# Two-stage transformer kernel: the late half of each attention unit moves to the end of its step

## The chip, the cores and the metric

The kernel runs on one core of a Trainium2 chip. The metric is the device time of one execution in microseconds (us), taken as the median of several runs.

## What is computed

The input is a sequence of 512 vectors of 1024 features. Two layers of a first block are applied (with 16 extra tokens in front, so 528), then two layers of a second block. Cut to what the change touches:

```python
# block 1, per layer: 4 heads of differential attention, causal, beside a recurrent branch
s = einsum('bqhcd,bkhcd->bhcqk', q, k) * scale          # two score maps c = 0, 1 per head
p = softmax(where(qpos >= kpos, s, -inf))
a = p[:, :, 0] - lam * p[:, :, 1]
o = einsum('bhqk,bkhe->bqhe', a, v)
h = h + concat([norm(o), norm(recurrent)]) @ w_out;  h = h + (silu(g) * u) @ w_down
# block 2, per layer: convolution, 6 heads of top-k attention (d), 6 heads of banded attention (c)
p = softmax(s + mask_or_bias);  y = einsum('bhqk,bkhd->bqhd', p, v)
x = layer_norm(ALPHA * x + concat([conv, y_d, y_c]) @ w_out)
# then attention over a memory of 256 tokens, and an MLP, each with a layer norm
```

## The kernel before, in words

**Products.** Activations are held with the features on the partitions. Every dense product is done as three float32r matmuls: high part of the weights by high part of the input (L511), low weights by high input (L514), high weights by low input (L517), in `dense` (L504). The weights arrive by DMA on the SP queue in pieces, ScalarE rounds the high part (`split_hi`, L985), VectorE subtracts the low part (`split_lo`, L1474), three buffers deep.

**Five programs and a table of steps.** Each engine has its own program, written out by hand; they meet through semaphores alone, and every engine works its list strictly in the order written. In the attention stage all five programs walk the same numbered steps, `STEPS1` = 80 steps in block 1 and steps 16 to 112 in block 2. In steps 0 to 63 of block 1 TensorE does in each step two chunks of an input projection (12 matmuls of 264 columns), in steps 64 to 66 and 75 to 79 chunks of the output projection, and in steps 67 to 74 no product at all. In block 2 a step holds 6 matmuls of 512 columns (steps 16 to 91), and from step 92 on the products for the memory's values, which call the units through `units` (L826).

**Units.** A unit is one block of 128 queries of one head (block 1: `UNITS1`, 20 per layer) or of one pair of heads (block 2: `UNITS2`, 24 per layer). They begin every 2 or 3 steps. A unit that begins at step s goes through the engines like this:

- step s: TensorE scores (L634, L636; L777, L779, L783 in block 2), VectorE maximum and its negative (L1615 to L1621; L1871, L1873);
- step s+1: ScalarE exponentials (L1077; L1259);
- step s+2: VectorE reciprocal of the sums (L1592; L1860), GpSimd scaling (L2111; L2163), and in block 1 VectorE's combination of the two maps, `combined` (L1700), which stands near the end of VectorE's step;
- step s+3: TensorE transposes of the probabilities into PSUM bank 6 (L604), or 6 and 7 (L746), then ScalarE's copy to SBUF, `turned_out` (L1061, L1065; L1250);
- step s+4: TensorE weighted sums of the values (L615; L755). In block 1 VectorE copies the result out, `o` (L1607). In block 2 ScalarE writes its high part, `part_hi` (L1241), in step s+4, and VectorE its low part, `part_lo` (L1854), at the front of step s+5.

On TensorE the transposes of unit s-3 and the weighted sums of unit s-4 stand first in a step, then come the scores, then the products, then the small matmuls of the other branches (`sums`, L536: statistics, rotation, gates; L794 rotation and L805 index scores in block 2). Before a bank is written again, `Banks.clear` (L494) waits for whoever empties it; so the transposes of a unit in block 2 also wait for `part_lo` of the unit before.

On ScalarE the copies of step s+3 (and `part_hi` of step s+4) stand ahead of the exponentials of the next unit:

```python
        if s - 3 in UNIT_AT1:
            w.wait_ge(*done("turned", l, u))          # L1058
            a = e.activation(K.turned1[u % 2]..., K.bank[6]..., ACT.Copy)
        if s - 1 in UNIT_AT1:
            w.wait_ge(*done("neg", l, u))             # L1071
            e.activation(K.probs1[u % 2][c]..., ACT.Exp, ...)
```

The output `o` of a head's last unit feeds the norm of that head: ScalarE squares it (`SUBSQ`, L1120, steps 36, 52, 57, 69), TensorE sums it (`SUBSTAT`, steps 39, 53, 59, 70).

Of the kernel before, what the change touches and what calls it, by code (L numbers as in the profile page):

```python
# [16 lines left out]
P = 128  # L17
# [559 lines left out]
def tensor_attention(e, w, K, B, l):  # L577
# [17 lines left out]
    for s in range(STEPS1):  # L595
        spare = ((s - 5) // 4) % 2
        D, d = K.psum[spare], (2 * spare, 2 * spare + 1)
        if s - 3 in UNIT_AT1:
            u, h, i = UNIT_AT1[s - 3]
            q0, rows, keys, blocks = unit1(i)  # L600
            B.clear(6)
            w.wait_ge(*done("combined", l, u))
            for j, (k0, n) in enumerate(blocks):
                mm = e.transpose(K.bank[6][0:n, j * rows:(j + 1) * rows], K.probs1[u % 2][0][0:rows, k0:k0 + n],  # L604
                                 ident[0:rows, 0:rows])
            mm.then_inc(*did("turned", l, u))
            B.emptied((6,), ("turned_out", l, u))
        if s - 4 in UNIT_AT1:
            u, h, i = UNIT_AT1[s - 4]
            q0, rows, keys, blocks = unit1(i)  # L610
            B.clear(7)
            w.wait_ge(*done("turned_out", l, u))
            w.wait_ge(*done("values", l, i))
            for j, (k0, n) in enumerate(blocks):
                mm = e.matmul(K.bank[7][:, 0:rows], K.v[0:n, j, h * P:(h + 1) * P],  # L615
                              K.turned1[u % 2][0:n, j * rows:(j + 1) * rows], start=j == 0, stop=j == len(blocks) - 1)
            mm.then_inc(*did("weighted", l, u))
            B.emptied((7,), ("o", l, u))
# [74 lines left out]
        if s == RECSTAT:  # L693
            B.clear(6, 7)
            w.wait_ge(*done("rec_sums", l, 3))
            sums(e, K.psum[3], ones, K.xc, T1).then_inc(*did("rec_stat", l))
            B.emptied((6, 7), ("rec_var", l))

# [36 lines left out]
def tensor_mixers(e, w, K, B, l):  # L735
# [3 lines left out]
    def step(s):  # L739
        if s - 3 in UNIT_AT2:  # L740
            u, kind, p, i = UNIT_AT2[s - 3]
            for c in range(2):
                B.clear(6 + c)
                w.wait_ge(*done("scaled", l, u, c))
                for j in range(i + 1):
                    mm = e.transpose(K.bank[6 + c][:, j * P:(j + 1) * P], K.probs2[u % 2][c][:, j * P:(j + 1) * P], ident)  # L746
                mm.then_inc(*did("turned2", l, u, c))
        if s - 4 in UNIT_AT2:
            u, kind, p, i = UNIT_AT2[s - 4]
            w.wait_ge(*done("tok", l, 3))  # L750
            for c in range(2):
                w.wait_ge(*done("turned2_out", l, u, c))
                at = TOK_V_CHK + (2 * p + c) * HEAD_DIM if kind == "c" else TOK_V_DSA
                for j in range(i + 1):
                    mm = e.matmul(K.bank[6 + c][c * HEAD_DIM:(c + 1) * HEAD_DIM, 0:P], K.tok[:, j, at:at + HEAD_DIM],  # L755
                                  K.turned2[c][:, j * P:(j + 1) * P], start=j == 0, stop=j == i)
                mm.then_inc(*did("weighted2", l, u, c))
                B.emptied((6 + c,), ("part_hi", l, kind, p, i, c), ("part_lo", l, kind, p, i, c))
        if s in UNIT_AT2:
# [13 lines left out]
            for c in range(2):  # L773
# [12 lines left out]
                B.emptied((4 + c,), ("exp2", l, u, c))  # L786

# [24 lines left out]
    for s in range(TOK_STEPS, MEM_STEP):  # L812
# [10 lines left out]
        beside(s)  # L823
    now = [MEM_STEP]

    def units():  # L826
        step(now[0])
        now[0] += 1
# [204 lines left out]
def scalar_attention(e, w, K, l):  # L1033
# [6 lines left out]
    for s in range(STEPS1):  # L1040
# [13 lines left out]
        if s - 3 in UNIT_AT1:  # L1054
            u, h, i = UNIT_AT1[s - 3]
            q0, rows, keys, blocks = unit1(i)
            full = sum(n == P for _, n in blocks) * rows
            w.wait_ge(*done("turned", l, u))  # L1058
            if u >= 2:
                w.wait_ge(*done("weighted", l, u - 2))  # L1060
            a = e.activation(K.turned1[u % 2][:, 0:full], K.bank[6][:, 0:full], ACT.Copy)  # L1061
            if blocks[-1][1] < P:
                n = blocks[-1][1]
                a.then_inc(*did("turned_out_part", l, u))
                a = e.activation(K.turned1[u % 2][0:n, full:full + rows], K.bank[6][0:n, full:full + rows], ACT.Copy)  # L1065
            a.then_inc(*did("turned_out", l, u))
# [34 lines left out]
        for n in range(REC_TILES):  # L1101
# [15 lines left out]
            if s == end + 4:  # L1117
                w.wait_ge(*done("inner", l, n))
                e.activation(K.g1, K.g1, ACT.Tanh, scale=math.sqrt(2.0 / math.pi)).then_inc(*did("gelu_tanh", l, n))
        if s in SUBSQ:  # L1120
# [97 lines left out]
def scalar_mixers(e, w, K, l):  # L1218
# [9 lines left out]
    for s in range(TOK_STEPS, STEPS2 + 5):  # L1228
# [4 lines left out]
        if s - 4 in UNIT_AT2:  # L1233
            u, kind, p, i = UNIT_AT2[s - 4]
            mix_at = (5 if kind == "c" else 2) + p
            for c in range(2):
                w.wait_ge(*done("weighted2", l, u, c))
                if u == 0:
                    w.wait_ge(*done("product", HID_FREE2[l]))
                own = slice(c * HEAD_DIM, (c + 1) * HEAD_DIM)  # L1240
                e.activation(K.hid_chunk(mix_at, T2)[0][own, i * P:(i + 1) * P], K.bank[6 + c][own, 0:P],  # L1241
                             ACT.Copy).then_inc(*did("part_hi", l, kind, p, i, c))
# [1237 lines left out]
```

## Time and profile before

| | |
|---|---|
| median of 3 runs | 3268.33 us (3263.41 to 3269.06) |
| the profiled execution's own time | 3267.59 us |
| its span, first to last instruction | 3265.8 us |
| instructions | 38797 |
| TensorE matmuls busy | 3025.8 us, 93% |
| TensorE weight loads busy | 2440.0 us, 75% |
| VectorE / ScalarE / GpSimd busy | 1644.1 (50%) / 1259.8 (39%) / 567.2 us (17%) |
| mean granted TensorE clock | 0.963 |
| chain of work that ended last | PE 80%, DVE 9%, issue 4%, ACT 4%, POOL 3% |

PE is TensorE, PEld its weight loads, DVE VectorE, ACT ScalarE, POOL GpSimd. Matmuls are pipelined, so two of them overlap in the records. "idle before" is the time an engine sat idle ahead of an instruction, with what released it. A granted clock of 1.00 is 2.4 GHz, 0.50 is 1.2 GHz.

### The profile page before, as it was taken

Reading aid. Unit: us, or ns where it says so; the run is one execution under the profiler, and the core shown is the slowest. Engines: PE = TensorE matmul, PEld = TensorE weight load, DVE = VectorE, ACT = ScalarE, POOL = GpSimd, SP = SyncE. Lnnn points to the kernel's source line nnn. Section 1 sums busy time; section 2 is a strip of 40 time slices with the busy share of each in tenths; the row PEclk is TensorE's granted clock in tenths of the full one; section 3 lists DMA queues with packets and bytes.
Section 4 is the critical chain, followed back from the end, with each engine's and each line's share of the span. In section 5 each row is a group of like instructions: output and inputs, shape, how many; then the busy total and the mean of one; then the engine's idle time right before and its main releaser. Section 6 shows DMA issues by size and latency. Waiting matters only on the chain.

```text
span 3265.8 us, 38797 instructions
## 1 busy us (share of the span) xinstructions
PE 3025.8 (93%) x15608; PEld 2440.0 (75%) x15608; DVE 1644.1 (50%) x2509; ACT 1259.8 (39%) x2104; POOL 567.2 (17%) x435
## 2 busy tenths in 40 slices
PE   8888999999888999999899979999798899979997
PEld 7667999997666788875557858888665577768885
DVE  5666545455575744545655454333555645353334
ACT  5454322234554422224343534333333335353333
POOL 2233000011232000002233240000412223230003
PEclk9998999999899999999899999999898899989999
DMA  3111232231112333331113212323211122123331
GB/s 133 33 39 46 87 91 90 90 99 57 33 33 62 98 98 95 92 100 36 43 55 97 85 57 91 97 92 95 68 52 36 46 91 97 59 71 97 95 93 63
DMA packets 71922, 244.33 MB, mean 75 GB/s; under 512 B 9152, under 2 KB 10816, under 8 KB 71744
## 3 DMA queue, kind: packets, MB, share of 16 engines
q1 hardware_dynamic: 66528, 235.50, 22.9%
q10 hardware_dynamic: 5216, 6.36, 0.6%
q8 instruction: 124, 2.03, 0.3%
q14 instruction: 54, 0.44, 0.0%
HBM read 239.73 MB, written 2.10 MB: 74 GB/s over the span
## 4 chain that ended last, share of the span: by engine, by line
PE 80%; DVE 9%; issue 4%; ACT 4%; POOL 3%; DMA 0%; ACTq 0%; DVEq 0%; POOLq 0%
PE psum L511 20%; PE psum L517 20%; PE psum L514 20%; PE psum L777 2%; PE psum L634 2%; PE psum L536 2%; PE psum L568 1%; PE psum L562 1%; PE psum L564 1%; PE psum L805 1%; POOL temp L2163 1%; PE psum L755 1%; PE psum L783 1%; PE psum L901 1%; PE psum L746 1%
## 5 line engine op out<-in xcount | busy, mean ns | idle before, releaser
L511 PE MATMUL psum<-act_hi_lo,weights_hi_lo 128*128 128x512 f32 (+2 forms) x2640 | 835.4, 354 | 19.1 <-ACT act_hi_lo L1371 16.9
L514 PE MATMUL psum<-act_hi_lo,weights_hi_lo 128*128 128x512 f32 (+2 forms) x2640 | 806.4, 343 | 1.9 <-DVE weights_hi_lo L1474 1.9
L517 PE MATMUL psum<-act_hi_lo,weights_hi_lo 128*128 128x512 f32 (+2 forms) x2640 | 805.3, 343 | 0.3
L1474 DVE TENSOR_TENSOR weights_hi_lo<-weights_float,weights_hi_lo 128x1024 fp32r<-128x1024 f32 (+2 forms) x446 | 571.8, 1283 | 263.8 <-ACT weights_hi_lo L985 262.7
L985 ACT ACTIVATE weights_hi_lo<-weights_float 128x1024 fp32r<-128x1024 f32 (+2 forms) x446 | 463.5, 1041 | 511.4 <-PE psum L517 438.6
L511 PEld LDWEIGHTS psum<-act_hi_lo,weights_hi_lo 128*128 128x128 f32 x2640 | 467.3, 193 | 89.8 <-issue 33.5
L511 PE MATMUL psum<-hidden_hi_lo,weights_hi_lo 128*128 128x512 f32 (+1 forms) x1488 | 502.9, 364 | 12.0 <-ACT hidden_hi_lo L1155 7.3
L517 PEld LDWEIGHTS psum<-act_hi_lo,weights_hi_lo 128*128 128x128 f32 x2640 | 465.0, 192 | 59.7 <-DVE act_hi_lo L1994 1.7
L514 PEld LDWEIGHTS psum<-act_hi_lo,weights_hi_lo 128*128 128x128 f32 x2640 | 466.4, 193 | 56.1 <-issue 2.6
L517 PE MATMUL psum<-hidden_hi_lo,weights_hi_lo 128*128 128x512 f32 (+1 forms) x1488 | 494.8, 359 | 1.7 <-POOL hidden_hi_lo L1731 1.2
L514 PE MATMUL psum<-hidden_hi_lo,weights_hi_lo 128*128 128x512 f32 (+1 forms) x1488 | 494.0, 358 | 1.1 <-DVE weights_hi_lo L1474 1.1
L511 PEld LDWEIGHTS psum<-hidden_hi_lo,weights_hi_lo 128*128 128x128 f32 x1488 | 266.6, 190 | 54.1 <-ACT hidden_hi_lo L1155 8.8
L517 PEld LDWEIGHTS psum<-hidden_hi_lo,weights_hi_lo 128*128 128x128 f32 x1488 | 265.3, 189 | 44.0 <-POOL hidden_hi_lo L1731 2.2
L514 PEld LDWEIGHTS psum<-hidden_hi_lo,weights_hi_lo 128*128 128x128 f32 x1488 | 266.3, 190 | 41.9 <-DVE weights_hi_lo L1474 2.0
L1737 DVE SCALAR_TENSOR_TENSOR x_residual<-x_residual,psum 128x512 f32<-128x512 f32 (+1 forms) x136 | 94.0, 691 | 338.4 <-PE psum L517 338.3
L2163 POOL TENSOR_SCALAR temp<-temp,small 128x512 f32<-128x512 f32 (+3 forms) x96 | 106.0, 1116 | 348.8 <-DVE small L1860 348.8
L2058 DVE TENSOR_TENSOR hidden_hi_lo<-temp,hidden_hi_lo 128x512 fp32r<-128x512 f32 x64 | 44.3, 692 | 221.2 <-ACT hidden_hi_lo L1441 221.2
L2196 POOL TENSOR_TENSOR temp<-x_residual 128x512 f32<-128x512 f32 x6 | 13.3, 2218 | 724.1 <-DVE x_residual L1737 724.1
L2099 POOL TENSOR_TENSOR temp<-temp 128x528 f32<-128x528 f32 (+1 forms) x24 | 34.0, 1416 | 434.4 <-ACT temp L1022 433.6
L1871 DVE TENSOR_REDUCE small<-psum 128x2 f32<-128x1024 f32 (+3 forms) x48 | 39.6, 825 | 138.6 <-PE psum L783 75.4
L1189 ACT ACTIVATE hidden_hi_lo<-temp 128x528 fp32r<-128x528 f32 (+1 forms) x44 | 28.1, 639 | 204.4 <-DVE temp L1773 204.4
L1435 ACT ACTIVATE temp<-psum 128x512 f32<-128x512 f32 x64 | 38.2, 597 | 172.2 <-PE psum L517 172.2
(246 smaller groups left out, 3541.5 us busy)
## 6 DMA issues: line engine op xcount, KB each, us to landing
weights_float<-in_w_ff SPq DMA_DIRECT2D x128, 512.0 KB, 3.6
weights_float<-in_w_gu SPq DMA_DIRECT2D x88, 512.0 KB, 3.5
weights_float<-in_w_in SPq DMA_DIRECT2D x70, 512.0 KB, 3.5
weights_float<-in_w_down SPq DMA_DIRECT2D x32, 448.0 KB, 3.3
weights_float<-in_w_out SPq DMA_DIRECT2D x16, 512.0 KB, 3.5
weights_float<-in_w_down SPq DMA_DIRECT2D x16, 512.0 KB, 3.5
weights_float<-in_w_mv SPq DMA_DIRECT2D x16, 512.0 KB, 3.3
weights_float<-in_w_mix SPq DMA_DIRECT2D x16, 512.0 KB, 3.3
```

Of the source, the lines that this page charges most:

```text
L511: e.matmul(slot[:, place:place + c1 - c0], w_hi[:, col], x_hi[:, c0:c1], start=first, stop=False)
L514: e.matmul(slot[:, place:place + c1 - c0], w_lo[:, col], x_hi[:, c0:c1], start=False, stop=False)
L517: mm = e.matmul(slot[:, place:place + c1 - c0], w_hi[:, col], x_lo[:, c0:c1], start=False, stop=final)
L536: mm = e.matmul(slot[:, place:place + c1 - c0], weights, moving[:, c0:c1], start=first, stop=final)
L634: e.matmul(slot[0:rows, k0:k1], K.q[half, h, q0:q0 + rows], K.k[half, h, k0:k1], start=True, stop=not k0 <= q0 < k1)
L777: e.matmul(bank[:, 0:keys], q[half, q0:q0 + P], k[half, 0:keys], start=True, stop=False)
L985: e.activation(K.parts(n)[0][:, 0:cols], K.staged(n)[:, 0:cols], ACT.Copy).then_inc(*K.did("hi", n))
L1474: e.tensor_tensor(lo[:, 0:cols], K.staged(n)[:, 0:cols], hi[:, 0:cols].bitcast(F32), ALU.subtract).then_inc(*K.did("lo", n))
L1737: e.scalar_tensor_tensor(along(x, width), along(x, width), alpha, across(K.psum[slot], width), ALU.mult, ALU.add).then_inc(*K.did(*mark))
L1871: e.reduce_max(top[:, 0:2], both, AX.X).then_inc(*did("max_score2", l, u))
L2058: e.tensor_tensor(lo, K.relu[f % 3][:, 0:T2], hi.bitcast(F32), ALU.subtract).then_inc(*did("hid_lo2", l, f))
L2163: e.tensor_scalar(prob, prob, m["small"][u % 4][:, 6 + c:7 + c], None, ALU.mult).then_inc(*did("scaled", l, u, c))
```

## The change

Nothing is added or removed: the same instructions are issued, some in another place of their engine's list.

- TensorE, block 1: the transposes of unit s-3 and the weighted sums of unit s-4 go from the front of a step to its end, behind scores, products and all `sums`.
- TensorE, block 2: the same two parts go into a function `turn`, called after `beside(s)`; in the steps of the memory's values it is called directly after `step`, so behind the scores and ahead of the products.
- ScalarE, block 1: `turned_out` goes behind the exponentials, the roots, the gates and the GELU parts of the step, ahead of the squares of the norms and of `split_hi`.
- ScalarE, block 2: `part_hi` and `turned_out` go behind the exponentials, the tile's eviction and the index ReLU.
- VectorE, block 1: `o` is done one step later (s-5 in place of s-4).

```diff
     for s in range(STEPS1):                                  # tensor_attention
         ...
-        if s - 3 in UNIT_AT1:
-            B.clear(6)
-            w.wait_ge(*done("combined", l, u))
-            for j, (k0, n) in enumerate(blocks):
-                mm = e.transpose(K.bank[6]..., K.probs1[u % 2][0]..., ident[...])
-            mm.then_inc(*did("turned", l, u))
-            B.emptied((6,), ("turned_out", l, u))
-        if s - 4 in UNIT_AT1:
-            B.clear(7)
-            w.wait_ge(*done("turned_out", l, u))
-            w.wait_ge(*done("values", l, i))
-            ...
-            mm.then_inc(*did("weighted", l, u))
-            B.emptied((7,), ("o", l, u))
         if s in UNIT_AT1:
             ... (scores, then products, statistics, rotation, gates)
         if s == RECSTAT:
             ...
+        if s - 3 in UNIT_AT1:
+            ... (the same lines)
+        if s - 4 in UNIT_AT1:
+            ... (the same lines)
@@ tensor_mixers
     def step(s):
-        if s - 3 in UNIT_AT2:
-            ... (transposes, L740 to L747)
-        if s - 4 in UNIT_AT2:
-            ... (weighted sums, L748 to L758)
         if s in UNIT_AT2:
             ...
+    def turn(s):
+        if s - 3 in UNIT_AT2:
+            ... (the same lines)
+        if s - 4 in UNIT_AT2:
+            ... (the same lines)
         ...
         beside(s)
+        turn(s)
     def units():
         step(now[0])
+        turn(now[0])
         now[0] += 1
@@ scalar_attention
-        if s - 3 in UNIT_AT1:
-            ... (turned_out, L1054 to L1066)
         if s - 1 in UNIT_AT1:
             ... (exponentials, then roots, gates, GELU)
+        if s - 3 in UNIT_AT1:
+            ... (the same lines)
         if s in SUBSQ:
@@ scalar_mixers
-        if s - 4 in UNIT_AT2:
-            ... (part_hi, L1233 to L1242)
-        if s - 3 in UNIT_AT2:
-            ... (turned2_out, L1243 to L1251)
         if s - 1 in UNIT_AT2:
             ... (exponentials, tile eviction, index ReLU)
+        if s - 4 in UNIT_AT2:
+            ... (the same lines)
+        if s - 3 in UNIT_AT2:
+            ... (the same lines)
@@ vector_attention
-        if s - 4 in UNIT_AT1:
-            u, h, i = UNIT_AT1[s - 4]
+        if s - 5 in UNIT_AT1:
+            u, h, i = UNIT_AT1[s - 5]
             w.wait_ge(*done("weighted", l, u))
             e.tensor_copy(K.q[:, h, q0:q0 + rows], K.bank[7][:, 0:rows]).then_inc(*did("o", l, u))
```

## Rows read from the trace of the kernel before

**Rows 1.** Who waited for whom, TensorE, whole run: us in total, times, longest.
```profile
PE psum L604 <- DVE arena L1700: 60.2, 38, 3.8
...
PE psum L746 <- DVE hidden_hi_lo L1854: 14.9, 8, 2.9
PE psum L746 <- POOL temp L2163: 13.7, 16, 1.7
PE psum L746 <- issue: 9.4, 4, 3.3
```
**Rows 2.** Busy time in stretches: PE, PEld, DVE, ACT, POOL busy, clock, DMA share, GB/s.
```profile
85.00:280.00 195.00, 159.57 (x956) 124.82 (x955) 124.39 (x225) 102.23 (x193) 61.57 (x46) 0.94 0.11 34
792.00:992.00 200.00, 163.61 (x956) 126.72 (x954) 126.67 (x228) 102.46 (x193) 61.26 (x46) 0.93 0.11 35
1458.00:1583.00 125.00, 118.42 (x486) 69.18 (x484) 65.74 (x165) 46.49 (x118) 25.49 (x22) 0.96 0.14 44
1583.00:1650.00 67.00, 57.96 (x239) 37.01 (x238) 44.09 (x107) 23.89 (x75) 17.11 (x19) 0.88 0.14 44
1650.00:1700.00 50.00, 45.62 (x205) 27.18 (x204) 29.05 (x58) 23.43 (x56) 16.91 (x13) 0.93 0.12 37
2420.00:2470.00 50.00, 50.00 (x208) 28.39 (x206) 30.59 (x87) 22.23 (x60) 10.65 (x11) 1.00 0.11 37
2470.00:2595.00 125.00, 107.66 (x431) 66.09 (x431) 76.01 (x178) 41.81 (x119) 32.36 (x32) 0.85 0.12 41
2595.00:2640.00 45.00, 41.43 (x204) 26.91 (x203) 21.66 (x40) 21.85 (x48) 16.55 (x11) 0.95 0.17 53
```
**Rows 3.** Timeline of TensorE around the longest wait of block 1.
```profile
129.09 0.41 PE L517 MATMUL psum<-act_hi_lo,weights_hi_lo 128*128 128x264 f32 x2
129.33 0.41 PE L511 MATMUL psum<-act_hi_lo,weights_hi_lo 128*128 128x264 f32 x2
...
134.03 0.33 PE L604 MATMUL psum<-consts,arena 128*128 128x128 f32 x1 [3.81 <-DVE arena L1700]
...
138.81 0.64 PE L517 MATMUL psum<-act_hi_lo,weights_hi_lo 128*128 128x264 f32 x2
139.25 0.64 PE L511 MATMUL psum<-act_hi_lo,weights_hi_lo 128*128 128x264 f32 x2
```
**Rows 4.** Timelines of VectorE, TensorE and ScalarE around one unit's hand-over.
```profile
147.92 0.17 DVE L1621 TENSOR_SCALAR small<-small 128x2 f32<-128x2 f32 x1
...
150.96 0.66 PE L604 MATMUL psum<-consts,arena 128*128 128x128 f32 x4 [2.56 <-DVE arena L1700]
...
151.65 0.60 ACT L1061 ACTIVATE temp<-psum 128x512 f32<-128x512 f32 x1 [7.25 <-PE psum L604]
152.27 1.28 ACT L1077 ACT_TABLE_LOAD   x1
153.56 0.58 ACT L1077 ACTIVATE arena<-psum,small 128x384 f32<-128x384 f32 x1
```
**Rows 5.** Timelines of TensorE and VectorE around one wait of block 2.
```profile
1568.15 0.39 PE L514 MATMUL psum<-act_hi_lo,weights_hi_lo 128*128 128x512 f32 x1
1568.38 0.39 PE L517 MATMUL psum<-act_hi_lo,weights_hi_lo 128*128 128x512 f32 x1
...
1572.91 1.51 PE L746 MATMUL psum<-consts,temp 128*128 128x128 f32 x6 [3.28 <-issue]
...
1572.53 0.60 DVE L1854 TENSOR_TENSOR hidden_hi_lo<-psum,hidden_hi_lo 64x128 fp32r<-64x128 f32 x2
```
**Rows 6.** Timelines, end of block 1's attention stage, layer 0: ScalarE and VectorE.
```profile
278.17 0.64 ACT L1119 ACTIVATE temp<-temp 128x528 f32<-128x528 f32 x1
...
279.38 0.70 DVE L1663 SCALAR_TENSOR_TENSOR temp<-temp 128x528 f32<-128x528 f32 x1
280.11 0.71 DVE L1665 SCALAR_TENSOR_TENSOR arena<-temp,arena 128x528 f32<-128x528 f32 x1
```

**Rows 7.** Groups of instructions by line, ScalarE's table loads at the exponentials of block 1.
```profile
L1077 ACT ACT_TABLE_LOAD x12 | 15.4, 1283 | 0.2
```

More of the change, by code:

```diff
@@ L697, in tensor_attention @@
             B.emptied((6, 7), ("rec_var", l))
+        if s - 3 in UNIT_AT1:
+            u, h, i = UNIT_AT1[s - 3]
+            q0, rows, keys, blocks = unit1(i)
+            B.clear(6)
+            w.wait_ge(*done("combined", l, u))
+            for j, (k0, n) in enumerate(blocks):
+                mm = e.transpose(K.bank[6][0:n, j * rows:(j + 1) * rows], K.probs1[u % 2][0][0:rows, k0:k0 + n],
+                                 ident[0:rows, 0:rows])
+            mm.then_inc(*did("turned", l, u))
+            B.emptied((6,), ("turned_out", l, u))
+        if s - 4 in UNIT_AT1:
+            u, h, i = UNIT_AT1[s - 4]
+            q0, rows, keys, blocks = unit1(i)
+            B.clear(7)
+            w.wait_ge(*done("turned_out", l, u))
+            w.wait_ge(*done("values", l, i))
+            for j, (k0, n) in enumerate(blocks):
+                mm = e.matmul(K.bank[7][:, 0:rows], K.v[0:n, j, h * P:(h + 1) * P],
+                              K.turned1[u % 2][0:n, j * rows:(j + 1) * rows], start=j == 0, stop=j == len(blocks) - 1)
+            mm.then_inc(*did("weighted", l, u))
+            B.emptied((7,), ("o", l, u))
     width = T1 if l + 1 < DEPTH else T2
@@ L1119, in scalar_attention @@
                 e.activation(K.g1, K.g1, ACT.Tanh, scale=math.sqrt(2.0 / math.pi)).then_inc(*did("gelu_tanh", l, n))
+        if s - 3 in UNIT_AT1:
+            u, h, i = UNIT_AT1[s - 3]
+            q0, rows, keys, blocks = unit1(i)
+            full = sum(n == P for _, n in blocks) * rows
+            w.wait_ge(*done("turned", l, u))
+            if u >= 2:
+                w.wait_ge(*done("weighted", l, u - 2))
+            a = e.activation(K.turned1[u % 2][:, 0:full], K.bank[6][:, 0:full], ACT.Copy)
+            if blocks[-1][1] < P:
+                n = blocks[-1][1]
+                a.then_inc(*did("turned_out_part", l, u))
+                a = e.activation(K.turned1[u % 2][0:n, full:full + rows], K.bank[6][0:n, full:full + rows], ACT.Copy)
+            a.then_inc(*did("turned_out", l, u))
         if s in SUBSQ:
@@ L1232, in scalar_mixers @@
             e.activation(K.tok[:, i, :], K.bank[4 + i][:, 0:TOK_COLS], ACT.Copy).then_inc(*did("tok", l, i))
-        if s - 4 in UNIT_AT2:
[L1234 to L1242, printed above, removed]
-        if s - 3 in UNIT_AT2:
-            u, kind, p, i = UNIT_AT2[s - 3]
-            keys = (i + 1) * P
-            for c in range(2):
-                w.wait_ge(*done("turned2", l, u, c))
-                if u > 0:
-                    w.wait_ge(*done("weighted2", l, u - 1, c))
-                e.activation(K.turned2[c][:, 0:keys], K.bank[6 + c][:, 0:keys], ACT.Copy).then_inc(
-                    *did("turned2_out", l, u, c))
         if s - 1 in UNIT_AT2:
```

72 lines of the change are left out of this document (34 added, 38 removed).

## The prediction

> **What bounds the kernel now.** I read four views. The page's chain that ended last gives 80% of the span to TensorE, and its busy share is 93%: the time is TensorE's own work plus what it waits for. The view of who waited for whom on TensorE then says what for. The longest entry is the transposes of block 1 (L604), which wait for VectorE's combination of the two maps (L1700): 60.2 us in 38 waits, at most 3.8 us each, of 40 units. Three further entries are the transposes of block 2 (L746): 14.9 us for VectorE's low part of the unit before (L1854), 13.7 us for GpSimd's scaling (L2163), and 9.4 us put down to "issue", in all 38.0 us in 28 waits [rows 1]. The second entry in that view, L860 of the layer norms, is not touched by the change.
>
> The third view, busy time in stretches, places this in the unit stages: in block 1 TensorE is idle for 195 - 159.57 = 35.4 us and 200 - 163.61 = 36.4 us, in block 2 for 6.6 + 9.0 + 4.4 us in one layer and 17.3 + 3.6 us in the other, 112.7 us together. The granted clock there is 0.94, 0.93, 0.96, 0.88, 0.93, 0.85 and 0.95. The stretch from 2420 to 2470 us, which has units and no wait, is 50.00 us busy at 1.00 [rows 2]. So the waits, not the small matmuls of the units, go with the lower clock. The fourth view, the timeline, shows one such place: after 3.81 us of idle time a pair of products is issued every 0.44 us instead of every 0.24 us, that is at 1.2 in place of 2.4 GHz, and this is so still 5 us later [rows 3].
>
> Why the transposes are late can be read from one hand-over. At 148.1 us unit 6 has its negative maximum, all that its exponentials need. ScalarE does them at 153.56 us, since ahead of them in its list stands the copy of unit 5's transposes (151.65 us), those stand behind TensorE's 2.56 us of idle time for unit 5's combination, and a table load of 1.28 us is ahead of the exponentials too [rows 4]. So each late unit delays the next: combination, transposes, copy, exponentials, combination. On TensorE the scores of the following unit stand behind the same wait when both are in one step.
>
> **The change part by part.** No instruction is added or taken away, and no DMA issue changes its place relative to what it waits for; SP's queue waits for the rounded weights, which ScalarE still writes at the end of its step, four steps or more ahead of use.
>
> *Transposes of block 1 behind the products.* Between the old place and the new lie at least the 12 products of the step: six pairs at 0.24 us [rows 3], 1.46 us. In the steps with a statistic, rotation or gate about 1 us more lies between, and where units begin three steps apart the next scores too; I count neither. The 38 waits average 1.58 us [rows 1]; taking 1.46 us from each of them, one by one in the timeline, and nothing from what is shorter, leaves 14.5 us of 60.2, most of it in the nine waits over 2.4 us; 45.7 us go. The bounds are 0, if the combination comes later by just as much, and all 60.2 us, since the exponentials now go ahead of the copy and the combination comes earlier. I take the sum by the products alone: it is the part of the cover that is in every step.
>
> *Transposes of block 2 behind scores and products.* Six products at 0.23 us are 1.4 us [rows 5]. Taking that from each of the 28 waits leaves 10 us; 28 us go. With the scores of the same step as cover too, which follow directly behind the transposes at all the waits for L1854, 36 us would go. Against that stands that the weighted sums, from which the low part is made, move back by a step's products as well. So I take 28 us, with the bounds 0 and 38.0. The last units, whose transposes stand beside the memory's values, get no products as cover, only scores where there are any; their waits are of 0.9 us (the 16 for L2163 average 0.86) [rows 1].
>
> *Weighted sums at the end of the step.* They wait for ScalarE's copy, issued behind TensorE's end of the step before, and have a full step of products as cover again. Who waits for them: in block 1 VectorE's copy o, moved one step back with them, and then a head's norm. Heads 0 to 2 have one step or more between o and its square. For head 3 there are no products left as cover (steps 67 to 74): o now stands behind the last GELU's two multiplications, 0.70 and 0.71 us, and the copy of the transposes behind one tanh of 0.64 us [rows 6]. That is at most 2 x (1.4 + 0.6) = 4 us in two layers; but the same tanh and multiplications come that much sooner and head the recurrent branch, which ends last (its sum stands behind head 3's). So it can also win as much; I take 0.
>
> *ScalarE's exponentials first.* What is passed is one or two copies of 0.6 us and, above all, their wait. The covering effect is in the bounds above. The number of table loads: in rows 4 the load stands between a copy and the exponentials, so the copy needs none of its own and none is added. The load costs 1.28 us from the end of the copy to the start of the exponentials [rows 4]. The Trainium skill, "ScalarE: Activation LUTs", section "What ACT_TABLE_LOAD costs", puts a switch at 2.66 us, with a drain of 1.38 us behind the load. The trace does not show that drain. By the page's figure, an estimate, each of the 12 loads that stand at the exponentials [rows 7] would eat 1.38 us more of their lead, and 17 us less would go in block 1: 3194 us.
>
> *New waits.* What is idle in these stages and is not for the transposes is 112.7 - 98.2 = 14.5 us (gates, scores and statistics that wait for ScalarE or VectorE). The long waits gave those engines time to catch up. VectorE is busy 124.4 of 195 us and 126.7 of 200 us, and 76.0 of 125 us in the worst stretch of block 2 [rows 2]; with some 30 us less per layer it would be at 75%. I double the other waits: 14.5 us lost. Bounds: nothing, or all the 74 us won so far (VectorE then sets the pace).
>
> *The clock.* What the throttle took in these stretches is length times (1 - clock): 11.7 + 14.0 + 5.0 + 8.0 + 3.5 + 18.8 + 2.3 = 63.3 us [rows 2]. Part of that fell in idle time, and waits of 1 to 2 us that remain may keep some of it. I take half, 31.7 us, between 0 and 56 us. The upper bound uses the products' own rows, 0.24 against 0.44 us, so that a microsecond at the lower clock loses 45% and not half [rows 3]. The Trainium skill, "TensorE: Matmul & The Clock Gate", section "Terms", says the penalty is the throttled time times one half; by that rule the upper bound would be 63 us.
>
> **Sum.** 45.7 + 28 - 14.5 + 31.7 = 90.9 us less than the profiled execution's own 3267.6 us: 3176.7 us. The median of the runs stands 0.7 us above that execution, so 3177 us. A measurement of this kernel can tell 0.2%, 6.5 us, from no change.
>
> **The rivals.**
> (A) *VectorE and ScalarE set the pace.* Then the transposes still wait, or the scores, gates and statistics do in their place. For it: a share of 75% leaves little slack where five lists are worked strictly in order. Against it: 59 to 66% of the time now [rows 2], and much of ScalarE's idle time is in front of the copy alone, 7.25 us before one [rows 4]. Half of the waits and a quarter of that clock: 37 - 14.5 + 16 = 38 us, 3230 us.
> (B) *The chain gets loose altogether.* Exponentials earlier by 3 to 5 us per unit take all 98 us of waits, the others stay at 14.5 us, and 45 us of clock come back: 143 us, 3125 us. For it: unit 6's exponentials, run at 153.56 us, could have run at 148.1 + 1.3 us, 4 us sooner [rows 4].
> (C) *The edit moves the wait and nothing else:* the combination comes a step later relative to TensorE, the reported waits at L604 and L746 keep 98 us. 3268 us. The 5 us that the exponentials gain speak against it.
> (D) *Slower.* In block 2 VectorE's low part stands at the front of its step and now waits for weighted sums at the very end of TensorE's step; behind it in VectorE's list are the maximum, the top-k search and `split_lo`. In block 1 ScalarE is held in the same way by the copy at the end of its step, ahead of `split_hi`. If that hold is a chain with no slack, each of the 88 units costs one step's products, 88 x 1.44 = 127 us, against the 98 us of waits that go: 29 us slower, 3297 us. It decides from the point where VectorE has less slack per unit than a step's products; now it has 125 - 76.0 = 49 us [rows 2] for the 12 or 13 units that fall into that stretch at about 10 us each, 4 us per unit where it is busiest, so I hold it unlikely.
>
> **How the numbers follow.** Forecast 0.63, A 0.18, B 0.10, C 0.04, D 0.05. The forecast's own range is 3145 to 3215 us: between the halves of the clock's and the waits' bounds. To hold eight in ten the range goes towards A and B: 3130 to 3234 us. C fills "same", D and nothing else "slower": faster 0.91, same 0.04, slower 0.05.
>
> **What would show it.** Right: in the profile after, L604's and L746's waits are at 25 us or less together; TensorE's idle time in the stage of block 1 is under 20 us per layer; ScalarE's idle time before L1061 no longer stands ahead of an exponential whose maximum is done; the clock is at 0.97 or more in the unit stages. VectorE's busy time is unchanged, its share of block 1's stage near 75%. A would show as new waits of L634, L536 and L604 on VectorE or ScalarE of 50 us and more; D as VectorE idle before L1854 for ScalarE's L1241 by over 50 us. The prediction is wrong if the waits go and the time does not, or if the dense stages outside, which I leave unchanged, move.

## The result and the profile after

The changed kernel takes 3128.59 us (median of four runs, 3125.47 to 3129.34), the kernel before 3265.87 us beside it (3259.32 to 3269.06). The ratio is 0.958, 95% interval 0.9563 to 0.9598: 137 us faster. The prediction said 3177 us with a range of 3130 to 3234 us. The sign was right, the size was not, and the median lies just below the range. The profiled execution took 3128.11 us, its span is 3126.3 us.

The first lines of the page of the kernel after, busy time, share and instructions of each engine:

```profile
span 3126.3 us, 38793 instructions
...
PE 2971.1 (95%) x15604; PEld 2417.0 (77%) x15608; DVE 1643.0 (53%) x2509; ACT 1261.1 (40%) x2104; POOL 567.7 (18%) x435
```

VectorE, ScalarE and GpSimd do the same work in the same time. TensorE's idle time falls from 3265.8 - 3025.8 = 240.0 us to 155.2 us, by 84.8 us, and its busy time, for the same products, by 54.7 us. These two make up the 139.5 us of the span. The mean granted clock goes from 0.963 to 0.976.

Who waited for whom on TensorE, kernel after (us in total, times, longest):

```profile
PE psum L864 <- POOL temp L2207: 39.2, 6, 7.9
...
PE psum L683 <- DVE arena L1704: 11.7, 11, 3.1
...
PE psum L613 <- ACT arena L1068: 8.3, 6, 3.6
...
PE psum L776 <- POOL temp L2167: 3.1, 4, 0.9
```

L683 is the old L604, L776 the old L746, L613 the scores of block 1 (L634 before), and L864 the sums of the layer norms (L860 before). The transposes' waits, 60.2 + 38.0 us in 66 waits [rows 1], are 14.8 us in 15. The scores of block 1 wait 8.3 us for the exponentials, 2.4 us before. The layer norms' 39.2 us are what they were.

Busy time in stretches, kernel after, columns as in [rows 2]: the unit stages of block 1 in both layers, then those of block 2.

```profile
85.00:250.00 165.00, 152.44 (x952) 121.25 (x951) 125.78 (x225) 103.00 (x194) 62.11 (x46) 0.96 0.13 39
760.00:935.00 175.00, 158.66 (x965) 124.72 (x963) 131.92 (x235) 107.49 (x201) 63.89 (x47) 0.95 0.13 40
...
1394.00:1612.00 218.00, 213.94 (x996) 135.28 (x997) 143.26 (x338) 100.15 (x259) 65.05 (x57) 1.00 0.17 53
2309.00:2513.00 204.00, 197.76 (x949) 128.33 (x949) 139.53 (x324) 98.29 (x247) 61.10 (x55) 1.00 0.19 61
```

Block 2 is the surprise: stretches at 0.96, 0.88, 0.93, 0.85 and 0.95 [rows 2] (the whole stages before, 1394 to 1700 us and 2400 to 2660 us, are at 0.94 and 0.91) have become two whole stages at 1.00. Block 1 is at 0.96 and 0.95, 0.94 and 0.93 before. What is left there has two larger items in each layer, a wait of 3.0 to 3.1 us at the transposes and the one seen in the timelines of TensorE and then ScalarE, kernel after:

```profile
222.28 0.44 PE L683 MATMUL psum<-consts,arena 16*128 16x16 f32 x5 [0.25 <-DVE arena L1704]
226.34 1.05 PE L613 MATMUL psum<-arena 64*128 64x256 f32 x2 [3.61 <-ACT arena L1068]
...
223.26 1.04 ACT L989 ACTIVATE weights_hi_lo<-weights_float 128x1024 fp32r<-128x1024 f32 x1
224.32 1.28 ACT L1068 ACT_TABLE_LOAD   x1
225.61 0.58 ACT L1068 ACTIVATE arena<-psum,small 128x384 f32<-128x384 f32 x1
```

The scores wait 3.61 us for exponentials that stand behind the rounding at the end of ScalarE's step before and behind a table load. The exponentials are first in their step, not first in ScalarE's list.

### The profile page after: what moved, and what is told of

It is laid out like the page before. It is cut to its first block, busy times and chain, and to the rows that moved or that the text cites. A ratio compares the mean times of both kernels' runs of the same rounds, so it can differ in the third digit from the quotient of the medians.

```text
span 3126.3 us, 38793 instructions
## 1 busy us (share of the span) xinstructions
PE 2971.1 (95%) x15604; PEld 2417.0 (77%) x15608; DVE 1643.0 (53%) x2509; ACT 1261.1 (40%) x2104; POOL 567.7 (18%) x435
## 4 chain that ended last, share of the span: by engine, by line
PE 83%; DVE 7%; issue 4%; ACT 3%; POOL 3%; DMA 0%; ACTq 0%; DVEq 0%; POOLq 0%
PE psum L511 21%; PE psum L517 21%; PE psum L514 21%; PE psum L758 2%; PE psum L536 2%; PE psum L613 2%; PE psum L568 1%; PE psum L562 1%; PE psum L564 1%; PE psum L807 1%; PE psum L785 1%; ACT weights_hi_lo L989 1%; PE psum L905 1%; PE psum L917 1%; PE psum L764 1%
## 5 line engine op out<-in xcount | busy, mean ns | idle before, releaser
L511 PE MATMUL psum<-act_hi_lo,weights_hi_lo 128*128 128x512 f32 (+2 forms) x2640 | 823.1, 349 | 17.3 <-ACT act_hi_lo L1375 14.7
L514 PE MATMUL psum<-act_hi_lo,weights_hi_lo 128*128 128x512 f32 (+2 forms) x2640 | 798.1, 340 | 1.9 <-DVE weights_hi_lo L1478 1.9
L517 PE MATMUL psum<-act_hi_lo,weights_hi_lo 128*128 128x512 f32 (+2 forms) x2640 | 797.4, 340 | 0.3
L511 PEld LDWEIGHTS psum<-act_hi_lo,weights_hi_lo 128*128 128x128 f32 x2640 | 462.0, 191 | 86.1 <-issue 29.3
L517 PEld LDWEIGHTS psum<-act_hi_lo,weights_hi_lo 128*128 128x128 f32 x2640 | 459.0, 189 | 58.6 <-DVE act_hi_lo L1998 1.7
L514 PEld LDWEIGHTS psum<-act_hi_lo,weights_hi_lo 128*128 128x128 f32 x2640 | 459.7, 190 | 56.6 <-issue 3.1
L562 PE MATMUL psum<-weights_hi_lo,act_hi_lo 128*128 128x512 f32 (+1 forms) x208 | 84.2, 405 | 21.0 <-ACT weights_hi_lo L989 10.0
```

The costliest lines, as they stand in the source:

```text
L511: e.matmul(slot[:, place:place + c1 - c0], w_hi[:, col], x_hi[:, c0:c1], start=first, stop=False)
L514: e.matmul(slot[:, place:place + c1 - c0], w_lo[:, col], x_hi[:, c0:c1], start=False, stop=False)
L517: mm = e.matmul(slot[:, place:place + c1 - c0], w_hi[:, col], x_lo[:, c0:c1], start=False, stop=final)
L562: e.matmul(bank, act[:, 0, here], w_hi[:, wk], start=k == 0, stop=False)
```

## The experiments

Two kinds of theory were open. P: the gain is *cover*, a step's products between the two ends of each link of a unit's chain. S: the gain comes from *ScalarE's order*, exponentials no longer behind a late copy. Beside them K, on the clock: idle TensorE costs a lower clock afterwards. All idle and busy times below are TensorE's, from the page of each profiled execution. In two kernels that execution is not a typical one: in `act_only` it is one of the two slowest of four (3312.05 us of 3294.66 to 3312.3), in `act_old_b2` the fastest (3184.81 us of 3184.81 to 3208.54), so the idle and busy times of these two are rough.

**The blocks one by one.** `b1_only` takes the three functions of block 1 from the kernel after and leaves block 2 as before, `b2_only` the reverse.

```diff
 # b1_only: the kernel before, with
+tensor_attention, scalar_attention, vector_attention of the kernel after
 # b2_only: the kernel before, with
+tensor_mixers, scalar_mixers of the kernel after
```

> The change in block 1 alone (all three engines), block 2 as before. The stage lengths of the two profiles give block 1 62.9 us of the 137.8 us of span. If the blocks gain each on its own: 3266 - 63 = 3203 us. If a part of what block 2 shows comes from block 1's earlier end (weights further ahead, another phase of the clock), this run gains 80 us or more. The transposes of block 2 keep their 38 us of waits either way.

> The change in block 2 alone. Gaining on its own: 3266 - 75 = 3191 us, waits at the transposes 3 us in place of 38 us, and the time at the lower clock in the two unit stages falls from 75 us to none: 35 us of waits and 37 us of clock. The rival, that the clock there comes back for another reason than the waits, would leave part of those 75 us although the waits are gone (3210 us and more).

Measured: 3205.02 us, ratio 0.9816 (0.979 to 0.9841), and 3191.0 us, ratio 0.9773 (0.9749 to 0.9797), where before has a median of 3268.7 us. So 64 and 78 us, both as expected: they add up to 141 us against 137 for both. The blocks don't touch each other within that, and block 2, which I had put behind block 1, gives more. Idle time falls by 48.4 and 37.7 us, busy time by 16.9 and 38.7 us: in block 2 more than half of the gain is busy time.

**ScalarE's order alone.** TensorE and VectorE as before.

```diff
 # the kernel before, with
+scalar_attention, scalar_mixers of the kernel after
```

> ScalarE's lists as after (exponentials first), TensorE and VectorE as before. Theory P (the products behind which the transposes go are the cover): little, 5 to 20 us less than before, since the transposes still stand at the front of their step. Theory S (the chain through ScalarE was the cause: late copy, late exponentials, late combination): the waits at block 1's transposes fall from 60 to under 25 us and the time by 50 us or more.

Measured: 3306.05 us, ratio 1.0112 (1.0074 to 1.015): slower by 37 us, and both theories missed. Who waited for whom in this kernel, on TensorE and, in the last two rows, on ScalarE and VectorE:

```profile
PE psum L604 <- DVE arena L1700: 59.8, 38, 3.6
...
PE psum L755 <- ACT temp L1282: 13.7, 14, 1.2
...
PE psum L746 <- ACT hidden_hi_lo L1273: 6.8, 6, 1.2
...
PE psum L615 <- ACT arena L1118: 5.4, 2, 2.8
PE psum L615 <- ACT arena L1114: 5.2, 6, 1.2
...
ACT arena L1064 <- DVE small L1621: 79.0, 26, 6.6
...
DVE arena L1607 <- PE psum L615: 36.5, 18, 4.2
```

The transposes of block 1 wait as long as before, 59.8 us, although the exponentials (L1064) are no longer late: ScalarE now stands idle 79.0 us for the maximum that they need (L1621), 19.9 us before. VectorE's wait for them (L1592) falls from 16.6 to 1.2 us, but in its place VectorE stands idle 36.5 us in front of `o` (L1607), 15.3 us before, and the combination stands behind `o` in its list. So late exponentials were one hold among several, and to take this one away alone takes nothing from the transposes' waits. The weighted sums (L615, L755), for which `o` waits, now wait for the copy. Why, ScalarE's and TensorE's timelines of the same kernel show:

```profile
1516.86 0.49 ACT L1264 ACTIVATE temp<-psum 128x384 f32<-128x384 f32 x1 [9.10 <-PE psum L805]
1517.24 0.87 ACT L1282 ACTIVATE temp<-psum 128x384 f32<-128x384 f32 x2
...
1517.78 2.03 PE L755 MATMUL psum<-temp,arena 128*64 128x128 f32 x12 [0.96 <-ACT temp L1282]
```

The copy (L1282) now stands behind the index ReLU (L1264), which waits for a product that TensorE issues late in its own step; the weighted sums stand first in TensorE's next step and catch the copy unfinished. A late copy needs a late consumer. (The timelines show block 2; that block 1 goes the same way is read from its waits.) Idle time rises by 17.8 us and busy time by 26.6 us.

**TensorE's order, with ScalarE's undone.** In block 2 this was run; in block 1, as the lists read, it can't be built whole. At step 38 TensorE's rotation needs the PSUM bank of the second score map of a 528-key unit, so it waits for that unit's exponentials; in ScalarE's old order these stand behind the copy of transposes that now end the same TensorE step. The two lists would wait for each other. This is read from the lists and was not tried. So `act_mostly_old_b1` keeps the new order in the steps ahead of which a 528-key unit begins.

```diff
 # act_old_b2: the kernel after, with
+scalar_mixers of the kernel before
 # act_mostly_old_b1: the kernel after, scalar_attention
+        if s - 3 in UNIT_AT1 and not (s - 1 in UNIT_AT1 and UNIT_AT1[s - 1][2] == 4):
+            ... (turned_out, ahead of the exponentials)
         if s - 1 in UNIT_AT1:
             ...
-        if s - 3 in UNIT_AT1:
+        if s - 3 in UNIT_AT1 and s - 1 in UNIT_AT1 and UNIT_AT1[s - 1][2] == 4:
             ... (turned_out, at its new place)
```

> The changed kernel with ScalarE's list of block 2 as before: the copies and part_hi ahead of the exponentials, which now hold ScalarE until the end of TensorE's step. Theory P: at most 10 us slower than the changed kernel (3129 to 3139 us). Theory S: most of block 2's 75 us is given back, 3170 us and more, with waits at the transposes for GpSimd's scaling.

> The changed kernel with ScalarE's copy of the transposed probabilities back ahead of the exponentials in block 1, except in the steps in which the unit two steps younger is one of 528 keys. Theory S (ScalarE's chain decides as in block 2, where the same undoing cost about 69 us): the exponentials wait for transposes that now stand at the step's end, each unit's scores wait for them; 3150 to 3200 us. Rival (in block 1 ScalarE's order only has to break the circle of waits at the 528-key units): 3125 to 3140 us.

Measured: 3197.94 us, ratio 0.979 (0.9755 to 0.9826), and 3177.7 us, ratio 0.9729 (0.9714 to 0.9745). Taking ScalarE's part away costs 69 us of block 2's 78, and 49 us of block 1's 64. Waits on TensorE, first in `act_old_b2`:

```profile
PE psum L758 <- ACT temp L1263: 24.4, 21, 1.5
```

and in `act_mostly_old_b1`:

```profile
PE psum L613 <- ACT arena L1081: 30.1, 20, 3.8
```

L1263 and L1081 are the exponentials. The transposes wait as little as in the kernel after, whatever ScalarE's order: 2.6 us against 3.1 us in block 2, 9.6 us against 11.7 us in block 1. But the scores of a later unit wait, for the PSUM bank that late exponentials still hold, and in block 1 the small matmuls of L536 wait 10.4 us for ScalarE (L1103). For block 1 that is the wait S named; for block 2 S had the time right, 3170 us and more, and the wait wrong, since it named the transposes. The clock in block 2's stages falls with waits that are all short. These are the stages in `act_old_b2`, with about as many products as in the stretches above:

```profile
1394.00:1640.00 246.00, 225.71 (x998) 142.15 (x1000) 146.48 (x337) 100.15 (x262) 65.52 (x57) 0.95 0.14 48
2337.00:2565.00 228.00, 207.65 (x921) 133.27 (x923) 139.93 (x323) 93.91 (x244) 62.40 (x55) 0.93 0.15 49
```

TensorE is idle 20.3 and 20.4 us. Beside the 12.0 us per layer for the exponentials the largest items are 2.7 us at L807 for ScalarE and one wait of 1.8 us (L562), the longest of all.

**How much cover is needed.** `w_front` leaves only the transposes at the end of the step. `scores_first` moves both parts behind the scores, not behind the products.

```diff
 # w_front: the kernel after
-        ... (weighted sums of s - 4, behind the transposes at the step's end)
+        ... (weighted sums of s - 4, ahead of the step's scores; both blocks)
 # scores_first: the kernel after
-        ... (transposes of s - 3, weighted sums of s - 4, at the step's end)
+        ... (the same, between the step's scores and its products; both blocks)
```

> The changed kernel with the weighted sums of both blocks put back at the front of their step, and only the transposes left at the step's end. Theory P (what the change bought is cover: each link of a unit's chain, VectorE or GpSimd to transposes, transposes to ScalarE's copy, copy to weighted sums, must have a step's products between its two ends): the copy of the transposed probabilities now has no products between the transposes at the end of one step and the weighted sums at the front of the next, so nearly each of the some 76 units in block 1 and 72 in block 2 waits about 0.5 to 1.5 us there; waits for the copy 60 to 150 us in all, the granted clock falls with them, 3180 to 3280 us. Rival C (only the transposes matter, the weighted sums were never late, 0.9 us of wait for the copy in the block-1 rows before and after): within 5 us of the changed kernel's 3129.

> The changed kernel with transposes and weighted sums moved ahead of the step's products, but still behind the step's scores, in both blocks. So the links keep a whole step between transposes and weighted sums, and the wait for the combined map is covered by the scores alone (1 to 2 us) in place of scores and products (6 to 8 us). Theory P: the waits of the transposes come back in part, at 1 to 1.5 us less each than in the kernel before, 20 to 50 us in all, 3150 to 3200 us. Rival R (the wait is a shift: what matters is only that the scores, which start the next unit's chain, are issued before the transposes can stall): within 10 us of 3129.

Measured: 3205.24 us, ratio 0.9816 (0.9798 to 0.9833), and 3223.08 us, ratio 0.9866 (0.9847 to 0.9885). `w_front` is 77 us slower than the kernel after: as P said, where no products lie between the transposes and what needs their copy, TensorE waits for the copy, though by less than I wrote (51 us in the rows below, of 60 to 150; the expectation also counted 76 and 72 units, where two layers have 40 and 48). Its waits:

```profile
PE psum L605 <- ACT temp L1118: 16.7, 16, 1.9
PE psum L605 <- ACT arena L1118: 14.2, 16, 1.7
PE psum L747 <- ACT temp L1286: 10.7, 40, 0.4
...
PE psum L605 <- ACT arena L1122: 9.8, 4, 4.4
```

`scores_first` is outside what either theory said, 3150 to 3200 us or within 10 us of 3129. Its waits:

```profile
PE psum L624 <- DVE arena L1704: 46.0, 32, 2.6
...
PE psum L785 <- ACT temp L1286: 13.7, 14, 1.2
```

Cover by the scores takes 14 of block 1's 60.2 us and 23 of block 2's 38.0 us (15.3 us are left at L776), and in block 2 a wait for the copy appears. The transposes' waits are 61 us in all, where P had said 20 to 50 us. Of the 137 us, this placement gets 46; having the products too ahead of transposes and weighted sums brings the other 91 to 95 (3223 against 3129 us). Rival R is out.

**VectorE's part.** `o`, the copy out of PSUM, back in its old step:

```diff
 # the kernel after, vector_attention
-        if s - 5 in UNIT_AT1:
-            u, h, i = UNIT_AT1[s - 5]
+        if s - 4 in UNIT_AT1:
+            u, h, i = UNIT_AT1[s - 4]
```

> The changed kernel with VectorE's copy of the weighted sum out of PSUM back in its old step, one step earlier, ahead of VectorE's other work of the step. Theory V (the copy now waits for weighted sums that stand at the end of TensorE's step, and VectorE's combined maps queue behind it, so the transposes wait again): 3140 to 3190 us, with the wait of the transposes in block 1 at 30 to 70 us. Rival (VectorE, at 52% busy, has the slack for it): 3125 to 3135 us.

Measured: 3175.92 us, ratio 0.9724 (0.9709 to 0.9738): 48 us slower than the kernel after, inside V's range. Who waited on TensorE, and then on VectorE, in this kernel:

```profile
PE psum L683 <- DVE arena L1704: 22.1, 16, 3.3
...
PE psum L613 <- ACT arena L1068: 11.3, 9, 3.6
```

```profile
DVE arena L1611 <- PE psum L694: 101.4, 35, 8.2
```

VectorE stands idle 101.4 us in front of `o`, 6.3 us in 5 waits in the kernel after, and what stands behind `o` in its list comes late. But the transposes' wait doubles only, to 22.1 us, where V expected 30 to 70 us. Of 48 us, 28.8 are idle time, in small pieces at several lines, and 21.6 are busy time. That VectorE is busy only half of the time does not help it: its list is in order.

**The clock by itself.** `filler` is the kernel *before* with products that compute nothing, in TensorE's idle time.

```diff
 # the kernel before, tensor_mixers
             u, kind, p, i = UNIT_AT2[s - 3]
+            if IDX_STEP + 3 * IDX_HEADS < s < MEM_STEP:
+                B.clear(3)
+                for _ in range(6):
+                    e.matmul(K.bank[3], K.act_chunk(0, T2)[0][:, 0:P], K.act_chunk(0, T2)[0], start=True, stop=True)
             for c in range(2):
```

> The kernel before with six extra products of 512 columns (results never used) put ahead of the block-2 transposes, in the steps in which those waited longest. They use the time in which TensorE stood idle, they give the units nothing. Theory K (the clock part: the low-clock stretches of the block-2 unit stages, 75 us of them in the two layers before and none after, are a consequence of TensorE's short idle waits, and half their length is lost): the granted clock in those stages rises to 0.97 or more, the products there shorten, and the time falls or stays, 3235 to 3275 us, though over 200 extra products are run. Rival (the clock's low stretches have another cause, for example the load of all engines together): the clock in those stages stays at 0.90 to 0.93 and the time rises by the extra products' 50 us or so less the 38 us of waits, 3275 to 3330 us.

Measured: 3252.48 us (3250.28 to 3261.3), ratio 0.9959 (0.9946 to 0.9972): 168 products more and 16 us *less*. The page's busy line of this kernel, its waits at the transposes, and three stretches of block 2:

```profile
PE 3037.7 (93%) x15776; PEld 2457.3 (76%) x15776; DVE 1644.6 (51%) x2509; ACT 1259.7 (39%) x2104; POOL 567.7 (17%) x435
```

```profile
PE psum L750 <- POOL temp L2167: 6.9, 10, 0.9
PE psum L750 <- issue: 3.8, 2, 1.9
PE psum L750 <- DVE hidden_hi_lo L1858: 3.0, 2, 1.5
```

```profile
1583.00:1650.00 67.00, 64.55 (x288) 42.57 (x288) 46.92 (x111) 24.70 (x76) 16.42 (x18) 0.95 0.13 44
1650.00:1700.00 50.00, 45.86 (x234) 30.36 (x233) 27.05 (x53) 23.37 (x54) 20.45 (x15) 1.00 0.15 49
...
2450.00:2575.00 125.00, 119.86 (x556) 78.97 (x556) 86.55 (x203) 46.17 (x134) 33.86 (x34) 1.00 0.13 43
```

The stretches that were at 0.88, 0.93 and 0.85 [rows 2] are at 0.95, 1.00 and 1.00 (the last one now lies 20 us sooner). At the 0.23 us from one such product to the next [rows 5] the extra ones need 168 x 0.23 = 39 us, yet busy time rises by 11.9 us only: by this estimate the kernel's own products take some 27 us less. The granted clock says the same: span times (1 - clock) falls from 120.8 to 94.3 us, by 26.5 us. The idle time falls by 26.6 us. Nothing of the units' chain was changed, so for these stages this shows K: the low clock went with idle times of at most 3.3 us [rows 1], and it goes when they are filled, even by products without use.

**The same trick on the kernel after.** Twenty f32 products of constants ahead of each layer norm's sums, and in `norm_end_fill` ten more ahead of the last transposes of block 1. `after_again` is the kernel after, unaltered, in the same session.

```diff
 # the kernel after, tensor_statistics
     B.clear(2 * slot, 2 * slot + 1)
+    for _ in range(20):
+        e.matmul(K.bank[2 * slot + 1][:, 0:P], ones, ones, start=True, stop=True)
 # norm_end_fill, also in tensor_attention
             B.clear(6)
+            if s == 67:
+                for _ in range(10):
+                    e.matmul(K.bank[6][:, 0:P], ones, ones, start=True, stop=True)
```

> The changed kernel once more, unaltered, as the measure for the three beside it: 3129 us within 5 us.

> The changed kernel with twenty extra products of 128 columns (constants by constants, results never used) ahead of the first product of each layer-norm sum, where TensorE stands idle 39.2 us in 6 waits and the granted clock is low for 10 to 17 us afterwards. Theory K (idle TensorE loses clock, whoever causes the idle time): the low-clock time behind these six places shrinks by most of some 80 us, half of it is time: 3090 to 3115 us. Rival (the low clock behind the layer norms comes from something else, as the four slow f32 products or the start of the next stage): 3125 to 3135 us. If the fill overshoots the waits, up to 3150 us.

> The same with ten more such products ahead of the last transposes of block 1, where TensorE waits 2.95 us with no products left. Theory K: a few us less than the kernel with the layer-norm fill alone (0 to 15 us, the low clock behind the block-1 stages being some 20 us per layer). Rival: the same time or up to 5 us more.

Measured: 3128.11 us, ratio 0.958 (0.9566 to 0.9594); 3123.97 us, ratio 0.9568 (0.9554 to 0.9583); 3120.94 us, ratio 0.9558 (0.9542 to 0.9574). That is 4 and 7 us, with intervals that overlap. The 4 us can't be told from nothing; the 7 us are at the edge of it (four runs from 3118.81 to 3125.13 us, beside 3126.07 to 3130.82 us for `after_again`). Neither is near K's 3090 to 3115 us. The stretches of two layer norms, and the wait behind the second one, in `after_again`:

```profile
1675.00:1700.00 25.00, 21.00 (x137) 17.72 (x138) 16.97 (x15) 14.04 (x22) 13.51 (x9) 0.86 0.29 98
1835.00:1870.00 35.00, 20.74 (x62) 14.02 (x63) 20.15 (x21) 18.63 (x26) 18.60 (x13) 0.76 0.07 25
...
1854.33 0.77 PE L511 MATMUL psum<-act_hi_lo,weights_hi_lo 128*128 128x512 f32 x1 [8.42 <-ACT act_hi_lo L1375]
```

and with the fill, in `norm_fill`:

```profile
1675.00:1700.00 25.00, 24.05 (x182) 21.60 (x181) 17.39 (x16) 15.55 (x23) 14.93 (x10) 1.00 0.32 111
1835.00:1870.00 35.00, 23.27 (x90) 16.81 (x89) 21.27 (x23) 20.45 (x29) 18.32 (x13) 0.85 0.06 22
...
1852.44 0.77 PE L511 MATMUL psum<-act_hi_lo,weights_hi_lo 128*128 128x512 f32 x1 [8.43 <-ACT act_hi_lo L1377]
```

At the first place the fill leaves 0.7 us of a wait of 5.3 us, and the clock stays at 1.00, so there the low clock does not come from the f32 sums themselves, as the rival had it. At the second it leaves 3.2 us of 7.7 us, and behind the sums stands a second wait, 8.4 us for ScalarE, which the fill does not reach: in both kernels the next products come every 0.43 us for the 6 us behind it, and then every 0.23 us. So much of the low clock stays: over the whole kernel, span times (1 - clock) falls from 68.7 to 59.3 us only, where K's expectation had some 40 us. What the fill does bring are faster sums. From the start of the first sum to the start of the last it saves 1.7, 1.5, 0.4, 1.6, 0.1 and 1.4 us at the six places, 6.6 us in all, and at the second place the next stage begins 1.9 us sooner (1852.44 against 1854.33 us), after the same wait of 8.4 us. The small gain is thus mainly low clock that stayed, behind waits that were filled in part or not at all. That a longer fill would bring the rest was not run.

## Why the prediction was wrong

The sum was 45.7 + 28 - 14.5 + 31.7 = 90.9 us; measured were 139.5 us in the profiled executions. Three terms were mis-sized, all to the same side.

- **Transposes: right in kind, short by 9.7 us.** 73.7 us were to go, 83.4 us went: 48.5 us in block 1 (45.7 expected) and 34.9 us in block 2 (28 expected). I counted the products as cover and nothing else. In block 2 the prediction itself has 36 us with the scores as cover too and sets it aside for the later low part; `scores_first` shows that cover, 23 of 38.0 us by the scores alone. The step that failed is "So I take 28 us". Whether the earlier exponentials took a part of it too is not shown: with them alone the transposes of block 1 keep 59.8 of 60.2 us (`act_only`), and with them undone the waits are as short as in the kernel after (9.6 and 2.6 us), but TensorE is then held in front of the scores.
- **New waits: wrong sign, 15.9 us.** The step that failed is "I double the other waits", 14.5 us more, since VectorE would be at 75%. It is, 125.78 of 165 us, and the scores wait 5.9 us more for exponentials; but all of TensorE's idle time outside the transposes is 84.8 - 83.4 = 1.4 us less. A busy share of 75% made no engine the bound.
- **The clock: short by 14 to 23 us, the largest of the three.** The step that failed is "I take half, 31.7 us", half of 63.3 us, since waits of 1 to 2 us would remain and keep some of it. By the rows of the same stages, two digits of clock each, block 1 goes from 25.7 to 15.4 us, less than half of it, and block 2 from 37.6 us to nothing. Span times (1 - clock) falls from 120.8 to 75.0 us, by 45.8 us; busy time falls by 54.7 us. The 8.9 us between them I can't assign; the third digit of the clocks leaves room for 3 of them. In block 2 only four waits of at most 0.9 us are left at the transposes, and none above 1.3 us elsewhere, and those stages are at 1.00. The upper bound of 56 us is slightly off too: 0.24 against 0.44 us makes it 57.5 us.
  The Trainium skill, "TensorE: Matmul & The Clock Gate", section "Terms", has the penalty as the throttled time times (1 - K/N), which is half of it at half rate; by that rule the whole kernel gives the 45.8 us, so the fall of the busy time lies above it by those 8.9 us.

9.7 + 15.9 + 23.0 = 48.6 us, which is the miss. Rival B (3125 us, chance 0.10) came within 4 us of the time, and that is partly luck: its 98 us of waits are 83.4 us, its unchanged other waits 1.4 us less, its 45 us of clock 54.7 us by the busy time, and the first and the last cancel. Its reason was the one hand-over in [rows 4] where exponentials could have run 4 us sooner. The holds did go, VectorE's for the exponentials from 16.6 to 0.5 us and for `o` from 15.3 to 6.3 us, but earlier exponentials alone do not do it, as `act_only` shows.

ScalarE's move I costed at nothing of its own ("The covering effect is in the bounds above"). That did not shift the sum, which was for all the moves together, but it is the deepest fault of the account: alone the move costs 37 us, and without it 49 us (block 1) and 69 us (block 2) are lost, though the transposes no longer wait. What it does is keep the scores from waiting for late exponentials. VectorE's `o`, priced in the prediction only at head 3's end, is worth 48 us. Each of these parts is needed for the others, since each removes a place where a wait would otherwise go. That the sum came out no further off with both unpriced is luck.

Of the other rivals: A (3230 us) asked for 50 us of new waits, which did not come. C asked that the waits stay, they went. D asked for over 50 us of VectorE idle before the low part of block 2; it is 35.0 us in 30 waits, from 12.2 us in 14, so the hold exists, and it did not reach TensorE. This is the row of the view of waits on VectorE, kernel after:

```profile
DVE hidden_hi_lo L1858 <- ACT hidden_hi_lo L1277: 35.0, 30, 3.3
```

The tail of block 1, taken at 0, was not measured apart from the rest. The table load is again 1.28 us to the start of the exponentials (224.32 to 225.61 us in the timeline above), with nothing between its end and the exponentials.
The variant by the Trainium skill, "ScalarE: Activation LUTs", section "What ACT_TABLE_LOAD costs" (a drain of 1.38 us behind each load, 3194 us), has no support in this trace, and it moved the sum the wrong way.

Of what I said would show it: the waits of L683 and L776 are under 25 us, TensorE's idle time is under 20 us in each layer's stage of block 1 (12.6 and 16.3 us), VectorE's share is 76%; but the clock in block 1 is 0.95 to 0.96, not 0.97.

## What to carry to other kernels

When several engines work lists in order, as here, put work for the rest of a unit's chain behind independent work of the same step, on every engine of the chain at once: one engine's move alone can cost what the whole move brings. When you cost such a change, count the idle time twice on TensorE, once as waits and once as the clock lost behind them, here 84.8 and some 50 us; and short waits count when they are repeated: here 20 us of idle time in a stage, no wait above 1.8 us, went with a clock of 0.95 and 0.93. Where TensorE has to wait, products without use can be cheaper than standing idle: 16 us in the unit stages here, 4 to 7 us at the layer norms, where they reached only part of the waits. And a hold read from one hand-over need not be the only one: with the late exponentials gone, VectorE waited in front of `o` instead.

## What the hardware showed that I had not expected

That 168 extra products of 512 columns made a kernel 0.4% faster (0.9959, 0.9946 to 0.9972). That in every kernel here in which the moves changed the idle time, busy time for the same products went with it, though in no fixed proportion: -84.8 and -54.7 us for the change, +17.8 and +26.6 us for ScalarE's order alone, and against the kernel after +32.3 and +24.4 us when that order is undone in block 2, +35.1 and +13.6 us when it is mostly undone in block 1, +41.3 and +37.3 us in `w_front`, +28.8 and +21.6 us in `o_old`, +63.9 and +33.8 us in `scores_first`. And that in block 2 some twenty waits per layer of at most 1.8 us, 20 us of idle time, go with a stage's clock of 0.95 and 0.93, where the same stage with 4.1 and 6.2 us of idle time has 1.00.
